# Gate loads of the value stage issued by GpSimd instead of SyncE's queue, in a PEER block on one Trainium2 core

## The chip, the cores and the metric

The kernel runs on one core of a Trainium2 chip. The metric is the device time of one execution in microseconds (us), lower is better. The core has TensorE (PE, matrix products), VectorE (DVE), ScalarE (ACT), GpSimd (POOL) and SyncE (SP). DMAs are issued from the instruction streams of SyncE and GpSimd here, and are carried by the core's 16 DMA engines.

## What is computed

One layer of a hybrid encoder with 512 tokens of width 1024: a token mixer (stick-breaking attention and gated linear attention) and then a PEER channel mixer, whose last part is what the change touches. For each token, 8 heads pick 16 of 128 x 128 single-neuron experts by product keys:

```python
def block(args):
    hb, ib, gb = args
    u = expert_u[ib]
    act = jax.nn.gelu(jnp.einsum('td,thkd->thk', hb, u), approximate=False)
    vv = expert_v[ib]
    return jnp.einsum('thk,thkd->td', gb * act, vv)
```

So y(token) is the sum over its 128 picks of gate x gelu(h . u) x v. The result is gated, added to the residual and normalised.

## The kernel before

The kernel treats the first 128 tokens and the other 384 differently.

**Dense tokens (384).** All 16384 experts are computed for them, in 128 blocks of 128 experts. In the *up stage* block b takes 24 matmuls of 384 columns into one of two banks `ps_u` (`UpProducts.product`); ScalarE empties the bank with a gelu (`gelu`, L1198) into one of four tiles `u_act`, and SyncE stores that tile to DRAM as `activations[b]` (`store`, L1202). gelu(b) waits until the store of block b - 4, from the same tile, has landed. In the *value stage* (`experts`) the activations are loaded again (`load_act`), multiplied on VectorE by the gates (`weigh`, L2049), split into a high and a low part (`w_high` on ScalarE, L2001; `w_low` on VectorE, L2042), and multiplied by the block's rows of v, which are loaded and split too (L1995, L2055): 18 matmuls of 512 columns a block into `ps_y`. The gates of tokens that did not pick an expert are zero.

The gates stand in DRAM as `gate_tiles`. For 256 dense tokens GpSimd spreads them there with 256 indirect DMAs of 128 words each (`spread_gate`, L1467; semaphore `spread`); for the other 128 a one-hot product writes them and SyncE stores them (semaphores `g_stored`). `load_gates(g)` then brings the gates of four blocks (a "quad") into one of two tiles `gates`: 768 KB, 128 partitions x 12 pieces x 512 bytes. gates(g) may be overwritten when quad g - 2 has been weighed (`w_done`).

**Picked rows (the first 128 tokens).** GpSimd fetches, for each of the 128 picks q, one row of u and v for every token by an indirect DMA of 128 rows of 8 KB (`PickedRows.gather`, L1248) into one of four tiles `row`. VectorE takes the dot product with h (L1255), ScalarE the gelu and the gate (L1259, L1262), VectorE adds the weighed v to `y_row` (L1271). gather(q) waits until row q - 4 has been added. The table `ROW_PACE` says in which block of the program each row is used, up to block 248, which is block 120 of the value stage.

**Order.** Every engine runs its own program in order. Steps are counted by b for the up stage and by i = b - 128 for the value stage; step i of VectorE does w_low(i + 1), weigh(i + 2), at most one row, and the split of v(i + 2). The value stage's steps begin at i = -7 (`OPENING`), beside the last up blocks 121 to 127. There SyncE's program interleaves the last u loads and stores with the first loads of v, activations and gates. On GpSimd, spreads and gathers are interleaved by the numbers `SPREAD_AT`, `SPREAD_PACE` and `ROW_BLOCK`; the last spread stands after gather 51, and gathers 52 to 127 follow one another in the same function; the value stage's function for GpSimd is empty.

## Time and profile before

| | |
|---|---|
| median of 3 runs | 1533.53 us (1531.42 to 1534.49) |
| profiled execution, own time | 1531.92 us |
| its span in the trace | 1530.0 us |
| TensorE busy | 1486.6 us (97%) |
| VectorE busy | 1225.9 us (80%) |
| ScalarE busy | 690.9 us (45%) |
| GpSimd busy | 515.9 us (34%) |
| HBM traffic | 278 GB/s over the span |

Busy shares are averages over stages of different kinds: up to about 400 us the mixer and the first keys, then the up stage, and from 993 us on the value stage. Times in the rows are us from the span's start. In a timeline row stand start, length, engine, line, operation and tiles, and in square brackets the engine's idle time before it with what ended it; "issue" is idle time for which the profile shows no releaser. SPq is SyncE's queue of DMA issues: the length there is that of the issue, not of the transfer. Ends of matmuls are modelled, starts are recorded. Software DMAs (q0) are GpSimd's, hardware DMAs (q1) SyncE's.

### The profile page before, as it was taken

Reading aid. Unit: us, or ns where it says so; the run is one execution under the profiler, and the core shown is the slowest. Engines: PE = TensorE matmul, PEld = TensorE weight load, DVE = VectorE, ACT = ScalarE, POOL = GpSimd, SP = SyncE. Lnnn points to the kernel's source line nnn. Section 1 sums busy time; section 2 is a strip of 40 time slices with the busy share of each in tenths; the row PEclk is TensorE's granted clock in tenths of the full one; section 3 lists DMA queues with packets and bytes.
Section 4 is the critical chain, followed back from the end, with each engine's and each line's share of the span. In section 5 each row is a group of like instructions: output and inputs, shape, how many; then the busy total and the mean of one; then the engine's idle time right before and its main releaser. Section 6 shows DMA issues by size and latency. Waiting matters only on the chain.

```text
span 1530.0 us, 22267 instructions
## 1 busy us (share of the span) xinstructions
PE 1486.6 (97%) x7635; PEld 1304.7 (85%) x7635; DVE 1225.9 (80%) x2476; ACT 690.9 (45%) x1189; POOL 515.9 (34%) x439
## 2 busy tenths in 40 slices
PE   6999998999999999999999999999999999999997
PEld 4786666889999999999999999888888888888886
DVE  6775657477799988999988965678888888888887
ACT  5424755363443433434555553344443444434443
POOL 0000000001476777668788867211111111112100
PEclk8999999999999999999999999999999999999999
DMA  9693903045787666756869988999999999999993
GB/s 367 236 352 130 415 29 139 4 144 210 247 277 246 213 223 220 235 181 196 261 222 337 323 327 315 384 377 351 382 373 374 382 361 381 382 369 380 368 349 115
DMA packets 169904, 427.46 MB, mean 279 GB/s; under 512 B 21152, under 2 KB 105280, under 8 KB 149824
## 3 DMA queue, kind: packets, MB, share of 16 engines
q1 hardware_dynamic: 143168, 291.67, 54.8%
q0 software_dynamic: 26624, 134.37, 23.1%
q8 instruction: 61, 1.00, 0.3%
q14 instruction: 51, 0.42, 0.1%
HBM read 373.42 MB, written 52.56 MB: 278 GB/s over the span
## 4 chain that ended last, share of the span: by engine, by line
PE 68%; POOL 4%; DMA 3%; issue 3%; DVE 1%; ACT 0%; DVEq 0%; ACTq 0%; POOLq 0%
PE ps_y L2124 11%; PE ps_y L2126 11%; PE ps_y L2128 11%; PE ps_u L1188 9%; PE ps_u L1190 9%; PE ps_u L1189 9%; POOL gate_tiles L1467 3%; PE ps_q L1475 2%; PE ps_q L1477 2%; PE ps_q L1476 2%; DMA activations<-u_act 1%; DMA row<-in_uv_rows,row_index 1%; PE ps_s L1487 1%; PE ps_g L1821 1%; DMA gate_tiles<-gate_owed,gate_cell 1%
## 5 line engine op out<-in xcount | busy, mean ns | idle before, releaser
L1467 POOL DMA_INDIRECT gate_tiles<-gate_owed,gate_cell x256 | 350.0, 1367 | 129.8 <-issue 72.0
L1188 PE MATMUL ps_u<-h_hi,u_hi 128*128 128x384 f32 x1024 | 349.2, 341 | 7.9 <-ACT u_act L1198 7.6
L1190 PE MATMUL ps_u<-h_hi,u_lo 128*128 128x384 f32 x1024 | 346.6, 338 | 0.0
L1189 PE MATMUL ps_u<-h_lo,u_hi 128*128 128x384 f32 x1024 | 346.5, 338 | 0.0
L1248 POOL DMA_INDIRECT row<-in_uv_rows,row_index x128 | 158.5, 1238 | 510.5 <-DVE y_row L1271 426.6
L1995 ACT CAST v_hi<-v_raw 128x1024 fp32r<-128x1024 f32 x128 | 134.7, 1053 | 266.8 <-DMA v_raw<-in_v 149.8
L2124 PE MATMUL ps_y<-v_hi,w_hi 128*128 128x512 f32 x768 | 238.1, 391 | 0.3 <-DVE w_lo L2042 0.3
L2126 PE MATMUL ps_y<-v_lo,w_hi 128*128 128x512 f32 x768 | 237.4, 390 | 0.0
L2128 PE MATMUL ps_y<-v_hi,w_lo 128*128 128x512 f32 x768 | 237.3, 390 | 0.0
L1188 PEld LDWEIGHTS ps_u<-h_hi,u_hi 128*128 128x128 f32 x1024 | 194.5, 190 | 10.2 <-issue 8.9
L2055 DVE TENSOR_TENSOR v_lo<-v_raw,v_hi 128x1024 fp32r<-128x1024 f32 x128 | 156.2, 1220 | 58.5 <-ACT v_hi L1995 56.1
L1178 DVE TENSOR_TENSOR u_lo<-u_raw,u_hi 128x1024 fp32r<-128x1024 f32 x128 | 154.9, 1217 | 55.0 <-ACT u_hi L1171 52.4
L1189 PEld LDWEIGHTS ps_u<-h_lo,u_hi 128*128 128x128 f32 x1024 | 194.6, 190 | 0.6
L1190 PEld LDWEIGHTS ps_u<-h_hi,u_lo 128*128 128x128 f32 x1024 | 194.4, 190 | 0.0
L1271 DVE SCALAR_TENSOR_TENSOR y_row<-row,row_weights,y_row 128x1024 f32<-128x1024 f32 x127 | 163.0, 1284 | 22.9 <-ACT row_weights L1262 22.9
L1255 DVE CUSTOM_DVE_ANT_0 row<-row,h_row 128x1024 f32<-128x1024 f32 x128 | 155.9, 1218 | 26.8 <-DMA row<-in_uv_rows,row_index 26.6
L2128 PEld LDWEIGHTS ps_y<-v_hi,w_lo 128*128 128x128 f32 x768 | 144.3, 188 | 30.1
L2126 PEld LDWEIGHTS ps_y<-v_lo,w_hi 128*128 128x128 f32 x768 | 144.3, 188 | 29.9
L2124 PEld LDWEIGHTS ps_y<-v_hi,w_hi 128*128 128x128 f32 x768 | 143.5, 188 | 29.6 <-DVE v_lo L2055 0.7
L1198 ACT ACTIVATE u_act<-ps_u 128x384 f32<-128x384 f32 x128 | 62.5, 488 | 199.3 <-PE ps_u L1190 172.3
L1171 ACT CAST u_hi<-u_raw 128x1024 fp32r<-128x1024 f32 x128 | 133.4, 1043 | 2.9 <-DMA u_raw<-in_u 2.9
L366 DVE CUSTOM_DVE_ANT_0 w_ada<-w_ada,c_row 128x1024 f32<-128x1024 f32 x47 | 55.8, 1220 | 0.3 <-DMA w_ada<-in_w_ada 0.3
(321 smaller groups left out, 2074.6 us busy)
## 6 DMA issues: line engine op xcount, KB each, us to landing
u_raw<-in_u SPq DMA_DIRECT2D x128, 512.0 KB, 4.7
v_raw<-in_v SPq DMA_DIRECT2D x128, 512.0 KB, 8.3
activations<-u_act SPq DMA_DIRECT2D x128, 192.0 KB
gates<-gate_tiles SPq DMA_DIRECT2D x32, 768.0 KB, 10.1
w_ada<-in_w_ada SPq DMA_DIRECT2D x23, 1024.0 KB, 8.1
gate_tiles<-blank SPq DMA_DIRECT2D x4, 4096.0 KB, 30.2
act<-activations SPq DMA_DIRECT2D x64, 192.0 KB, 8.6
u_act<-activations SPq DMA_DIRECT2D x64, 192.0 KB, 8.2
```

The lines of the kernel that those rows point to most:

```text
L1178: dve.tensor_tensor(self.lo[n][:], self.raw[n][:], self.hi[n][:].bitcast(F32), ALU.subtract).then_inc(self.lo_done, 1)
L1188: pe.matmul(out, self.hi[n][:, k], hi, start=(k == 0), stop=False)
L1189: pe.matmul(out, self.hi[n][:, k], lo, start=False, stop=False)
L1190: last = pe.matmul(out, self.lo[n][:, k], hi, start=False, stop=(k == KD - 1))
L1248: pool.indirect_dma_start(out=self.row[n][:].rearrange("p a d -> p (a d)"), out_offset=None, in_=self.table, in_offset=bass.IndirectOffset ...
L1255: dve.tensor_tensor_reduce(u, u, h_row[:], 1.0, 0.0, ALU.mult, ALU.add, self.dots[:, q:q + 1]).then_inc(self.dotted, 1)
L1271: dve.scalar_tensor_tensor(self.y[:], v, col, self.y[:], ALU.mult, ALU.add).then_inc(self.added, 1)
L1467: pool.indirect_dma_start(out=g_dram, out_offset=bass.IndirectOffsetOnAxis(ap=picks.cell[:, b, j:j + 1], axis=0), in_=picks.owed[:, b, j:j ...
L2055: dve.tensor_tensor(v_lo[i % VS][:], v_raw[i % VS][:], v_hi[i % VS][:].bitcast(F32), ALU.subtract).then_inc(vlo, 1)
L2124: pe.matmul(out, hi, v_hi[i % VS][:, c], start=first, stop=False)
L2126: pe.matmul(out, hi, v_lo[i % VS][:, c], start=False, stop=False)
L2128: last = pe.matmul(out, lo, v_hi[i % VS][:, c], start=False, stop=end)
```

## The change

`load_gates` moves from SyncE's program to GpSimd's, which now has a function in the value stage: it waits for `g_stored` and for all spreads, and then issues the gathers from 52 on with the 32 gate loads between them. gates(g) stands behind the gathers whose turn (`gather_at`) comes before step 4(g - 1) - 1. SyncE no longer waits for the spreads. The tiles `gates` are allocated ahead of `v_raw` instead of behind `w_lo`. Nothing is computed differently.

```diff
@@ retrieval, gpsimd
-            while q < PICKS:
-                rows.gather(pool, q)
-                q += 1
-
-        def gather_at(q):
-
-            return 7 if q < rows.RING else ROW_BLOCK[q - rows.RING + 1] + 1
+            rows.early = q
@@ PickedRows
+    def gather_at(self, q):
+
+        return 7 if q < self.RING else ROW_BLOCK[q - self.RING + 1] + 1
@@ experts, tiles
+        gates = [sb(f"gates{n}", [P, G_TILES, QUAD, G_TOK]) for n in range(2)]
         v_raw = [sb(f"v_raw{n}", [P, D]) for n in range(VS)]
...
-        gates = [sb(f"gates{n}", [P, G_TILES, QUAD, G_TOK]) for n in range(2)]
@@ experts, sync
-            def load_gates(g):
-                if g >= 2:
-                    sp.wait_ge(w_done, QUAD * (g - 1))
-                src = g_dram.rearrange("(a p i t) o -> p a i (t o)", a=G_TILES, p=P, t=G_TOK)[:, :, g * QUAD:(g + 1) * QUAD]
-                sp.dma_start(gates[g % 2][:], src).then_inc(g_in[g % 2], 16)
-
...
                         for n in range(2):
                             sp.wait_ge(g_stored[n], 16 * (P // G_TOK // 2))
-                        sp.wait_ge(spread, 16 * SPREADS * PEER_HEADS)
-                        load_gates(0)
                         load_v(0)
...
-                    if i == 3 - OPENING:
-                        load_gates(1)
...
-                if i % QUAD == 2 and i + 6 < N_KEYS:
-                    load_gates((i + 6) // QUAD)
@@ experts, gpsimd
-            pass
+            def load_gates(g):
+                if g >= 2:
+                    pool.wait_ge(w_done, QUAD * (g - 1))
+                src = g_dram.rearrange("(a p i t) o -> p a i (t o)", a=G_TILES, p=P, t=G_TOK)[:, :, g * QUAD:(g + 1) * QUAD]
+                pool.dma_start(gates[g % 2][:], src).then_inc(g_in[g % 2], 16)
+
+            for n in range(2):
+                pool.wait_ge(g_stored[n], 16 * (P // G_TOK // 2))
+            pool.wait_ge(spread, 16 * SPREADS * PEER_HEADS)
+            q = rows.early
+            for g in range(N_KEYS // QUAD):
+                while q < PICKS and rows.gather_at(q) < N_KEYS + QUAD * (g - 1) - 1:
+                    rows.gather(pool, q)
+                    q += 1
+                load_gates(g)
+            while q < PICKS:
+                rows.gather(pool, q)
+                q += 1
```

In the rows of order below, a row is an instruction of one engine's program with its line, its tiles and, in brackets, the semaphores it waits for; "x4" is four alike in a row.

SyncE at the opening of the value stage, before: the u load and the store of step -7, and then the first loads of gates, v and activations between the stores of the last blocks.

```order
337 L1163 DMA u_raw<-in_u 128x1024 [waits u_lo_done]
338 L1202 DMA activations<-u_act 128x384 [waits u_act_done]
339 L1938 DMA gates<-gate_tiles 128x12x128 [waits gates_spread,g_stored1,g_stored0]
340 L1932 DMA v_raw<-in_v 128x1024
341 L1202 DMA activations<-u_act 128x384 [waits u_act_done]
342 L1944 DMA act<-activations 128x384 [waits act_stored0]
343 L1944 DMA act<-activations 128x384 [waits act_stored1]
344 L1932 DMA v_raw<-in_v 128x1024
345 L1202 DMA activations<-u_act 128x384 [waits u_act_done]
346 L1932 DMA v_raw<-in_v 128x1024
347 L1202 DMA activations<-u_act 128x384 [waits u_act_done]
348 L1938 DMA gates<-gate_tiles 128x12x128
```

The same place of SyncE's program with the change:

```order
337 L1163 DMA u_raw<-in_u 128x1024 [waits u_lo_done]
338 L1202 DMA activations<-u_act 128x384 [waits u_act_done]
339 L1930 DMA v_raw<-in_v 128x1024 [waits g_stored1,g_stored0]
340 L1202 DMA activations<-u_act 128x384 [waits u_act_done]
341 L1936 DMA act<-activations 128x384 [waits act_stored0]
342 L1936 DMA act<-activations 128x384 [waits act_stored1]
343 L1930 DMA v_raw<-in_v 128x1024
344 L1202 DMA activations<-u_act 128x384 [waits u_act_done]
345 L1930 DMA v_raw<-in_v 128x1024
346 L1202 DMA activations<-u_act 128x384 [waits u_act_done] x4
```

The two gate loads and the wait for `gates_spread` are gone; the store of block 120, row 341 before and 340 now, stands behind the load of v(0) alone.

GpSimd at the end of the spreads, before: the last spreads, then all the gathers that are left.

```order
146 L1467 DMA gate_tiles<-gate_owed,gate_cell 6291456x1 [waits u_mul] x6
147 L1248 DMA row<-in_uv_rows,row_index 128x2048 [waits row_added,row_indexed]
148 L1467 DMA gate_tiles<-gate_owed,gate_cell 6291456x1 [waits u_mul] x2
149 L1248 DMA row<-in_uv_rows,row_index 128x2048 [waits row_added,row_indexed]
150 L1467 DMA gate_tiles<-gate_owed,gate_cell 6291456x1 [waits u_mul] x4
151 L1248 DMA row<-in_uv_rows,row_index 128x2048 [waits row_added,row_indexed] x76
```

The same place with the change, where the gather with five semaphores is gather 52:

```order
149 L1248 DMA row<-in_uv_rows,row_index 128x2048 [waits row_added,row_indexed]
150 L1465 DMA gate_tiles<-gate_owed,gate_cell 6291456x1 [waits u_mul] x4
151 L1248 DMA row<-in_uv_rows,row_index 128x2048 [waits row_indexed,gates_spread,row_added,g_stored1,g_stored0]
152 L1248 DMA row<-in_uv_rows,row_index 128x2048 [waits row_added,row_indexed] x3
153 L1977 DMA gates<-gate_tiles 128x12x128
154 L1248 DMA row<-in_uv_rows,row_index 128x2048 [waits row_added,row_indexed] x2
155 L1977 DMA gates<-gate_tiles 128x12x128
156 L1248 DMA row<-in_uv_rows,row_index 128x2048 [waits row_added,row_indexed] x3
157 L1977 DMA gates<-gate_tiles 128x12x128 [waits mod_kept]
```

Gather 52 now stands behind the wait for the spreads, gates(0) behind gather 55, gates(1) behind gather 57, and from there on a gate load stands behind every two or three gathers. (`mod_kept` is the name that the semaphore of `w_done` first had.)

## Rows read from the trace of the kernel before

**Rows 1.** Windows, value stage: busy us and instructions of each engine, PEclk, DMA share, GB/s.

```profile
1000.00:1500.00 500.00, 500.00 (x2223) 414.33 (x2222) 422.19 (x577) 213.83 (x394) 82.23 (x68) 1.00 1.01 369
```

**Rows 2.** Waits of TensorE, whole program: us in total, times, longest.

```profile
PE ps_u L1188 <- ACT u_act L1198: 7.6, 5, 2.9
```

**Rows 3.** Timeline of TensorE at the stage change.

```profile
965.80 0.42 PE L1188 MATMUL ps_u<-h_hi,u_hi 128*128 128x384 f32 x1 [0.61 <-ACT u_act L1198]
...
978.02 0.34 PE L1189 MATMUL ps_u<-h_lo,u_hi 128*128 128x384 f32 x1
978.19 0.34 PE L1190 MATMUL ps_u<-h_hi,u_lo 128*128 128x384 f32 x1
981.44 0.66 PE L1188 MATMUL ps_u<-h_hi,u_hi 128*128 128x384 f32 x1 [2.91 <-ACT u_act L1198]
...
982.22 0.53 PE L1190 MATMUL ps_u<-h_hi,u_lo 128*128 128x384 f32 x1
...
987.34 0.40 PE L1188 MATMUL ps_u<-h_hi,u_hi 128*128 128x384 f32 x1
...
993.42 0.70 PE L2124 MATMUL ps_y<-v_hi,w_hi 128*128 128x512 f32 x2
```

**Rows 4.** Timeline of ScalarE, gelu(124).

```profile
980.81 0.49 ACT L1198 ACTIVATE u_act<-ps_u 128x384 f32<-128x384 f32 x1 [7.44 <-DMA activations<-u_act]
```

**Rows 5.** Timeline of SyncE's queue: gates(0) and the store of block 120.

```profile
959.41 0.50 SPq L1938 DMA_DIRECT2D gates<-gate_tiles  x1
...
960.77 7.47 SPq L1202 DMA_DIRECT2D activations<-u_act  x1
```

**Rows 6.** Timeline of VectorE: dot of row 52, weigh(0), w_low(0).

```profile
963.48 1.23 DVE L1255 CUSTOM_DVE_ANT_0 row<-row,h_row 128x1024 f32<-128x1024 f32 x1 [5.08 <-DMA row<-in_uv_rows,row_index]
...
982.88 0.56 DVE L2049 TENSOR_TENSOR act<-act,gates 128x384 f32<-128x384 f32 x1 [7.73 <-DMA act<-activations]
...
987.73 0.55 DVE L2042 TENSOR_TENSOR w_lo<-act,w_hi 128x384 fp32r<-128x384 f32 x1
```

**Rows 7.** Timeline of GpSimd: an earlier wait for spreads; last spread, gathers 52 and 55.

```profile
681.88 0.97 POOL L1467 DMA_INDIRECT gate_tiles<-gate_owed,gate_cell  x1 [0.30 <-issue]
687.41 0.97 POOL L1467 DMA_INDIRECT gate_tiles<-gate_owed,gate_cell  x1 [4.56 <-DMA gate_tiles<-gate_owed,gate_cell]
...
952.53 0.97 POOL L1467 DMA_INDIRECT gate_tiles<-gate_owed,gate_cell  x1 [0.30 <-issue]
953.80 1.97 POOL L1248 DMA_INDIRECT row<-in_uv_rows,row_index  x1 [0.31 <-issue]
...
966.69 1.17 POOL L1248 DMA_INDIRECT row<-in_uv_rows,row_index  x1 [7.34 <-DVE y_row L1271]
```

**Rows 8.** Software queue in 954:955 and in 958:959: packets, MB, share of 16 engines.

```profile
q0 software_dynamic: 32, 0.00, 2.4%
...
q0 software_dynamic: 10, 0.08, 24.3%
```

**Rows 9.** TensorE after two other waits; windows, columns as in rows 1.

```profile
952.48 0.41 PE L1188 MATMUL ps_u<-h_hi,u_hi 128*128 128x384 f32 x1 [1.64 <-ACT u_act L1198]
...
812.79 0.41 PE L1188 MATMUL ps_u<-h_hi,u_hi 128*128 128x384 f32 x1 [2.13 <-ACT u_act L1198]
...
814.00:815.00 1.00, 1.00 (x5) 1.00 (x5) 1.00 (x2) 0.91 (x1) 0.70 (x2) 0.50 0.85 125
```

**Rows 10.** By tile: landing of gate loads 940:1000; gate loads and gathers, value stage.

```profile
DMA to landing us min/median/max: 15.1/16.2/16.4
...
L1938 SPq DMA_DIRECT2D gates<-gate_tiles x29: 371/432/1122, 1016.5 to 1477.1; - x29
...
DMA to landing us min/median/max: 7.5/9.7/13.1
...
L1248 POOL DMA_INDIRECT row<-in_uv_rows,row_index x68: 936/1175/1972, 999.9 to 1469.2; - x68
...
DMA to landing us min/median/max: 7.2/8.9/10.9
```

More of the change, by code:

```diff
@@ L1446, in gpsimd @@
                     at = SPREAD_AT + SPREAD_PACE * g + (SPREAD_PACE - SPREAD_REST) * n / SPREADS
-                    while q < PICKS and gather_at(q) < at + (SPREAD_REST if n == 0 else 0):
+                    while q < PICKS and rows.gather_at(q) < at + (SPREAD_REST if n == 0 else 0):
                         rows.gather(pool, q)
```

## The prediction, before the changed kernel was run

> **What bounds the kernel now.** I read the windows first, then the waits of TensorE, then the timeline of each engine around the only place where TensorE still stands still. In the value stage TensorE is busy in 500.00 of 500 us at full clock, and the DMA engines are busy too (share 1.01) [rows 1]. So moving issues between queues can give nothing there; it can only take, if something comes so late that TensorE waits. Over the whole program, the longest wait of TensorE for one releaser is 7.6 us in five pieces, all for the gelu that empties a bank of the up products; the longest piece is 2.9 us [rows 2]. It lies where the up products end and the value products begin, and there the timeline shows three losses [rows 3]: 0.61 us before block 123 (965.80), 2.91 us before block 126 (981.44), and behind the second a half clock. Matmuls that start every 0.17 us at 978.02 to 978.19 start every 0.32 us at 982.22. From 981.44 to 987.34 there are 18 matmuls in 5.90 us, where 18 x 0.173 = 3.12 would do: 2.78 us lost. The first value product starts at 993.42.
>
> Who is late at block 126? gelu(124) starts at 980.81 after 7.44 us of idle time, for a store of activations [rows 4]: the ring of four makes it wait until block 120 is stored. The queue of SyncE shows why [rows 5]: gates(0) is issued at 959.41, and the store of block 120, which stands two places behind it, has an issue of 7.47 us. An issue of a plain load there is 0.4 us at the median [rows 10]. 768 KB in pieces of 512 bytes stand ahead of that store.
>
> The 0.61 us before block 123 have another cause. VectorE waits 5.08 us for row 52, until 963.48 [rows 6]; ScalarE stands in its own order behind that dot product, and gelu(121) behind ScalarE's step. TensorE starts 965.80 - 963.48 = 2.32 us after the row is in.
>
> **The change, part by part.** (1) SyncE no longer issues the 32 gate loads and no longer waits for the spreads; its wait for the dense gates' stores (`g_stored`) stays. At the stage change v(0) and the store of block 120 then go out from 959.4 on, with no 768 KB ahead of them. I take the 2.91 us wait and the 2.78 us of half clock behind it as gone: 5.7 us is all there is to win. Cover is ample: without the gates the store has from about 960 to 978 to land.
>
> (2) GpSimd now waits for `g_stored` and for all 256 spreads before gather 52, where it had gone straight on: the last spread starts at 952.53 and gather 52 at 953.80 [rows 7]. When is the last spread in? Earlier waits of this kind ended 5.53 us after the last spread's start (681.88 to 687.41); that gives 958.1, 4.3 us late. The queue of the software DMAs gives an earlier bound: it moves 32 packets of almost no bytes in 954 to 955, and the next ones, 8 KB each, are row 52's in 958 to 959 [rows 8], so the spread's data has gone by 955. I let its completion count 0.6 us behind that (my choice between nothing and the 3.1 us left to 958.1, near the low end because the packets are what is seen), and gather 52 goes out at about 955.6, 1.8 us late. I take row 52 in 1.4 us late, since its packets then share the engines with less, and keep 4.3 as the other end. Behind gather 52 stand 53, 54, 55 and gates(0); behind its landing stand VectorE's dot, ScalarE, gelu(121) and block 123. So the 0.61 us wait becomes 2.0.
>
> (3) Does a wait of 2.0 us halve the clock? After 1.64 us (952.48) it did not; after 2.13 us (812.79) it did, to 0.50 in 814 to 815 [rows 9]; after 2.91 us it did. So the place is open between 0 and 2.8 us. I take 1.0, a little under the middle.
>
> (4) gates(0) now stands behind gather 55. That waits for row 51's add and started at 966.69 [rows 7]; 1.4 us later and 1.2 + 0.3 us long, it lets gates(0) go at 969.6, where SyncE sent it at 959.41. Landing took 15.1 to 16.4 us at the stage change and 9.7 us at the median later [rows 10]: 979.3 to 986.0. From weigh(0) at 982.88 to the end of w_lo(0) at 988.28 VectorE takes 5.4 us [rows 6], so the first value product can start at 984.7 to 991.4. TensorE, by (1) to (3), is there at 993.4 - 5.7 + 1.4 + 1.0 = 990.1. Hidden for most of the range, so nothing is charged; at the late end it costs 1.3 us.
>
> (5) Price of issuing a gate load on GpSimd. The trace has no plain load on that engine. A load is 128 x 12 pieces of 512 bytes. From below: a gather of 128 rows is 1.175 us [rows 10]. From above: twelve times that, 14.1 us, if time follows the number of pieces. I take 5 us, nearer the gather: a spread of 128 single words takes 0.97 us, a gather of 128 rows of 8 KB 1.17 us [rows 7], so bytes hardly count and a fixed share is likely; how much of the 1.2 us grows with pieces stays open. In the value stage GpSimd is busy 82.23 us of 500 with 68 gathers [rows 1]; with 0.3 us between instructions 397 us are free for the 29 loads of that stretch, 13.7 us each. At 5 us it all lies beside other work.
>
> (6) Rows behind a gate load. A gather lands in 8.9 us [rows 10] and its dot product comes three rows of the pace later, some 20 us; 5 us of issue and about 4 us of a gate load's data ahead of it in the same queue still fit. Nothing charged. SyncE's loads of v no longer stand behind gates, which is worth nothing either, as TensorE waits for none of them.
>
> Sum: -2.91 - 2.78 + 1.4 + 1.0 = -3.3 us. Against the profiled execution's own 1531.92 us that is 1528.6; the median of the runs is 1533.53, 1.6 above it, so 1530.2 us is the forecast, 0.21% less. From no change a measurement of this kernel can tell about 0.2%, 3.1 us.
>
> **Rivals.** *The gain is given back at block 123 or is not there.* If row 52 comes 4.3 us late, the wait becomes 4.9 us with the whole half clock behind it: -5.7 + 4.3 + 2.8 = +1.4 us, 1534.9. Or the store lands late anyway, because the same bytes share the same 16 engines: then -0 + 1.4 to 2.4. Against that speaks that the issue itself was held for 7.47 us [rows 5]. The trace thus has a queue effect beside the sharing of engines. The Trainium skill (DMA: Bandwidth & Descriptors, section Issuing engines are not separate DMA queues) says that DMAs of all issuing engines interleave on the same 16 engines and that spreading them saves only the issue time, usually small; by that rule the result would be this rival, about 1534. The half way between forecast and this rival (whole half clock at block 123, row 1.8 late) gives -1.1 us, 1532.4.
>
> *GpSimd becomes the bound* (slower). If a gate load costs 14.1 us there, the stretch of 500 us needs 29 x 14.4 + 68 x 1.48 = 518 us: +18, less the 3.3, so 1548. It decides from 13.7 us a load. For it speaks that nothing in the trace shows so many pieces generated in software; against it, the fixed share in (5). The Trainium skill (SBUF — State Buffer, section Summary: rules for kernel authors) advises against this move: descriptors written by GpSimd starve while VectorE runs in its wide modes. VectorE is busy 422 us of 500 here [rows 1], yet 68 gathers had a median of 1175 ns and a maximum of 1972 [rows 10], so I see the starvation at 0.8 us at most.
>
> *gates(0) comes too late* (slower, milder). If generation takes 10 us and landing 11.5 us behind it (between the 9.7 and the 16.4 of [rows 10]), gates(0) is in at 969.6 + 21.5 = 991.1 and the first value product starts 5.4 us later, at 996.5, with a half clock behind a wait of 6 us: 996.5 - 993.4 + 2.8 = +5.9 us, 1539.
>
> *More than forecast.* No half clock at block 123 and row 52 hardly late: -5.7 + 1 = -4.7, down to 1527.
>
> **How the numbers follow.** Forecast as summed (gain 2.2 to 4.4 us): 0.42, of it 0.25 beyond 0.2%. More than that: 0.12. Given back or not there: 0.25. gates(0) too late: 0.09. GpSimd the bound: 0.12. Faster 0.25 + 0.12 = 0.37; same 0.17 + 0.25 = 0.42; slower 0.21. The range of the forecast alone is 1529 to 1531.5. The range that holds 8 in 10 goes from 1527 (all the gain but the row's delay) to 1538, short of the case in which GpSimd is the bound and of the worst of late gates.
>
> **What the changed profile would show.** Right: the store of block 120 issued in under 1.5 us; gelu(124) waiting for TensorE and no longer for a store; no wait of TensorE before block 126; gather 52 some 2 us behind its old place after the last spread and a wait of about 2 us before block 123; gate loads on GpSimd of some 5 us; the first value product about 3 us before 993.4; 500 of 500 us busy in the value stage. Wrong: TensorE waiting in the value stage for w_lo or v_lo; GpSimd busy over 90% there; gate loads near 1 us would not change the sum, near 14 would. The forecast also falls if the wait before block 123 grows past 3 us.

## The result, and the profile after

The change made the kernel slower: 1540.03 us at the median (1530.15 to 1545.18, 20 runs) against 1532.18 us (1524.27 to 1535.67, 20 runs), ratio 1.0045 with the interval 1.0031 to 1.0059. That is about 6.9 us (4.8 to 9.0) more, where 3.3 us less were forecast. 1540.03 lies above the range of 1527 to 1538. The profiled execution of the changed kernel took 1536.13 us, with a span of 1534.3 us (before 1530.0); it lies below the median of its kernel, so this trace need not show all of the 6.9 us. Here and below two executions of e14, of 1852 and 5243 us, are left out of the ratio.

The windows and TensorE's waits of the changed kernel, value stage first (busy us of PE, PEld, DVE, ACT, POOL; clock; DMA share; GB/s):

```profile
1000.00:1500.00 500.00, 496.29 (x2203) 410.04 (x2202) 423.35 (x575) 212.92 (x394) 113.46 (x98) 1.00 1.00 367
```

```profile
PE ps_u L1188 <- ACT u_act L1198: 8.8, 4, 5.5
...
PE ps_y L2127 <- DVE w_lo L2045: 4.0, 4, 2.6
```

The reader should see two things. TensorE, busy 500.00 of 500 us in [rows 1], now stands still for 3.7 us in the value stage, and the waits have a name, `w_lo`. The waits for gelu at the change of stages have grown from 7.6 to 8.8 us [rows 2], where they should have shrunk.

The timeline of the changed kernel at the change of stages, by engine (start, duration, what, idle time before it):

```profile
951.56 2.04 POOL L1465 DMA_INDIRECT gate_tiles<-gate_owed,gate_cell  x1 [0.30 <-issue]
958.97 0.98 POOL L1248 DMA_INDIRECT row<-in_uv_rows,row_index  x1 [5.37 <-issue]
...
970.60 1.18 POOL L1248 DMA_INDIRECT row<-in_uv_rows,row_index  x1 [8.13 <-DVE y_row L1275]
971.78 1.10 POOL L1977 DMA_DIRECT2D gates<-gate_tiles  x1
...
967.39 1.23 DVE L1259 CUSTOM_DVE_ANT_0 row<-row,h_row 128x1024 f32<-128x1024 f32 x1 [10.03 <-DMA row<-in_uv_rows,row_index]
...
981.89 0.56 DVE L2052 TENSOR_TENSOR act<-act,gates 128x384 f32<-128x384 f32 x1 [2.83 <-DMA gates<-gate_tiles]
...
958.72 0.50 SPq L1202 DMA_DIRECT2D activations<-u_act  x1
...
969.72 0.66 PE L1188 MATMUL ps_u<-h_hi,u_hi 128*128 128x384 f32 x1 [5.47 <-ACT u_act L1198]
...
973.67 0.34 PE L1188 MATMUL ps_u<-h_hi,u_hi 128*128 128x384 f32 x1
...
993.21 0.70 PE L2127 MATMUL ps_y<-v_hi,w_hi 128*128 128x512 f32 x2
```

The last spread starts at 951.56 and gather 52 only at 958.97, 7.4 us later; in [rows 7] it was 1.3 us. Row 52 is in at 967.39 instead of 963.48 [rows 6], gelu(121) stands behind it, and TensorE waits 5.47 us before block 123, with the granted clock at 0.50 in 970 to 973 (the lower level, 1.2 GHz) and short spacing again from 973.67. The other side of the exchange is there as well: the store of block 120 is issued in 0.50 us instead of 7.47 [rows 5], and no wait stands before block 126. Both together leave the first value product where it was, 993.21 against 993.42 [rows 3].

So the 4.3 us between the two profiled executions lie behind that point. From the first value product to the end of the span: 1534.3 - 993.21 = 541.1 us, before 1530.0 - 993.42 = 536.6 us. I call this the **tail** below. The loads of gates in the value stage, by their line:

```profile
L1977 POOL DMA_DIRECT2D gates<-gate_tiles x30: 1067/1084/1098, 1002.8 to 1482.2; - x30
...
DMA to landing us min/median/max: 7.5/11.3/12.9
```

One costs GpSimd 1.08 us, and they are in after 11.3 us at the median (9.7 in [rows 10]). VectorE never waits for them in this stretch. What comes late is something else. The queues of 1000 to 1500 us (packets, MB, share of the 16 engines), first of the changed kernel, then of the kernel before:

```profile
q0 software_dynamic: 16032, 94.90, 51.0%
q1 hardware_dynamic: 35188, 88.13, 48.2%
```

```profile
q1 hardware_dynamic: 82147, 112.78, 65.4%
q0 software_dynamic: 9792, 71.31, 35.1%
```

The same bytes go in far fewer packets. Over the whole program the hardware queue loses 143168 - 93504 = 49664 packets and the software queue gains 33280 - 26624 = 6656: by load and engine 97 packets before, 13 now, that is 96 packets of 512 bytes and one of 4 bytes before, and now 12 packets of 4096 bytes and one of 4 bytes by the sizes in the packet records: eight pieces of 512 bytes travel as one packet. And ScalarE, which casts v, waits for v more (us in total, times, longest; changed, then before):

```profile
ACT v_hi L1998 <- DMA v_raw<-in_v: 179.1, 68, 5.1
ACT v_hi L1998 <- PE ps_y L2131: 47.7, 31, 2.2
```

```profile
ACT v_hi L1995 <- DMA v_raw<-in_v: 149.8, 55, 5.4
ACT v_hi L1995 <- PE ps_y L2128: 76.6, 47, 2.2
```

Read the second row of each pair as spare time. Where the cast waits for TensorE to free a buffer, v is early. Where it waits for the transfer, v is late, and three buffers must cover it. In the kernel before 55 casts found v late; now 68 do. This is how it reaches TensorE, in the chain of waits of the changed kernel around its longest new wait:

```profile
1278.16 13.06 DMA v_raw<-in_v
...
1291.24 0.02 ACT v_hi L1998
...
1294.37 1.22 DVE v_lo L2058
1295.59 0.48 DVE w_lo L2045
1296.07 0.14 issue
1296.20 0.70 PE ps_y L2127 x2
```

And this is what GpSimd had put into the engines around the issue of that load of v:

```profile
1271.28 1.17 POOL L1248 DMA_INDIRECT row<-in_uv_rows,row_index  x1 [3.25 <-DVE y_row L1275]
1272.44 1.08 POOL L1977 DMA_DIRECT2D gates<-gate_tiles  x1
1277.77 1.21 POOL L1248 DMA_INDIRECT row<-in_uv_rows,row_index  x1 [4.24 <-DVE y_row L1275]
```

A load of v took 13.06 us, where the median is 8.3 in both kernels. TensorE had no product to do for 2.59 us.

### The profile page after: what moved, and what is told of

Read it like the earlier page. It is cut to its first block and busy times, and to the rows that moved or that the text cites. A ratio compares the mean times of both kernels' runs of the same rounds, so it can differ in the third digit from the quotient of the medians.

```text
span 1534.3 us, 22268 instructions
## 1 busy us (share of the span) xinstructions
PE 1486.0 (97%) x7635; PEld 1302.8 (85%) x7635; DVE 1227.6 (80%) x2476; ACT 690.3 (45%) x1189; POOL 547.2 (36%) x471
## 3 DMA queue, kind: packets, MB, share of 16 engines
q1 hardware_dynamic: 93504, 266.51, 48.8%
q0 software_dynamic: 33280, 159.54, 28.5%
## 6 DMA issues: line engine op xcount, KB each, us to landing
gates<-gate_tiles POOLq DMA_DIRECT2D x32, 768.0 KB, 11.3
```

## The experiments

All were timed in five rounds beside the kernel before. In each profile, one by kernel, I read the tail, and how long ScalarE waited for v between 1000 and 1500 us. Theory A says that the loss comes from two places and mostly from the value stage; theory B that it comes from gather 52 at the change of stages.

### The change taken apart

**e1_wait_later.** The changed kernel; GpSimd's waits stand behind gathers 52 to 55.

```diff
-            for n in range(2):
-                pool.wait_ge(g_stored[n], 16 * (P // G_TOK // 2))
-            pool.wait_ge(spread, 16 * SPREADS * PEER_HEADS)
             q = rows.early
...
+                if g == 0:
+                    for n in range(2):
+                        pool.wait_ge(g_stored[n], 16 * (P // G_TOK // 2))
+                    pool.wait_ge(spread, 16 * SPREADS * PEER_HEADS)
                 load_gates(g)
```

> The changed kernel, with GpSimd's waits for the spreads and the dense gates' stores moved behind gathers 52 to 55, right ahead of gates(0). Theory A (two places: the late gather 52 eats the gain at the stage change, and the value stage loses some 8 us on its own because gate loads in GpSimd's queue hold up the loads of v): gather 52 goes out 1 to 2 us after the last spread again, the wait before block 123 is back under 1 us, the first value product starts at about 988, and the total is some 5 us under the changed kernel's 1540, near 1535, 0.2% above before. Theory B (one place: the late row 52 is the whole loss and whatever follows is its echo): about 1527, 0.3% below before.

Measured: 1537.92 us, ratio 1.0036 (1.0015 to 1.0056); tail 542.3.

```profile
960.16 0.66 PE L1188 MATMUL ps_u<-h_hi,u_hi 128*128 128x384 f32 x1 [6.40 <-ACT u_act L1198]
...
960.22 2.04 POOL L1465 DMA_INDIRECT gate_tiles<-gate_owed,gate_cell  x1 [0.30 <-issue]
962.56 1.98 POOL L1248 DMA_INDIRECT row<-in_uv_rows,row_index  x1 [0.31 <-issue]
```

Gather 52 is free again, 2.3 us behind the last spread, and before block 123 TensorE waits 0.23 us, as theory A said. The wait of 6.40 us is another one: it stands before block 120 and ends before the last spread is issued, so the place of GpSimd's waits can't have made it. With it the first value product comes at 997.24 and not at 988. The time decides nothing between "0.2% above before" and the change's 0.45%: the interval holds both. Theory B's 1527 us is out.

**e2_wait_only.** The kernel before, with the wait for the spreads ahead of gather 52 and nothing else.

```diff
+            pool.wait_ge(spread, 16 * SPREADS * PEER_HEADS)
             while q < PICKS:
                 rows.gather(pool, q)
```

> The kernel before, with nothing but GpSimd's wait for all spreads put ahead of gather 52; the gate loads stay with SyncE. Theory A: gather 52 is 5 us late, TensorE waits some 5 us before block 123 with a half clock behind it, the store's delay before block 126 partly hides behind that; 3 to 6 us above before, 1535 to 1538, and TensorE still busy 500 of 500 us in the value stage. Theory B: the whole loss, 1540, with waits in the value stage.

Measured: 1534.10 us, ratio 1.0005 (0.9990 to 1.0020); tail 536.6. The wait alone costs nothing that can be measured, where theory A had 3 to 6 us for it: gather 52 went 2.4 us behind the last spread, not 5 us late, and TensorE does not wait before block 123. In this execution it waits 4.78 us at 954.80, again before block 120 and ahead of gather 52 (956.13), and later only 0.34 and 0.65 us where the kernel before waited 2.91. It looks as if a wait early in the change of stages took the place of a later one, but this early wait is not the edit's.

**e3_first_two.** Gates 0 and 1 and the waits as in the change; loads 2 to 31 stay in SyncE's loop.

```diff
-            for g in range(N_KEYS // QUAD):
+            for g in range(2):
...
+                if i % QUAD == 2 and i + 6 < N_KEYS:
+                    load_gates((i + 6) // QUAD)
```

> The change at the stage change alone: GpSimd waits for the spreads ahead of gather 52 and issues gates(0) and gates(1); the other 30 gate loads stand in SyncE's program as before (the two kinds on semaphores of their own). Theory A: the stage change is neutral, about 1532 as before, and TensorE is busy 500 of 500 us from 1000 on. Theory B: 1540, as the changed kernel.

Measured: 1535.61 us, ratio 1.0014 (0.9992 to 1.0036); tail 536.5. That may be nothing or up to 0.36%.

**e4_later_thirty.** The other half alone: change of stages as before, loads 2 to 31 taken out of SyncE's loop and put into GpSimd's.

```diff
-                if i % QUAD == 2 and i + 6 < N_KEYS:
-                    load_gates((i + 6) // QUAD)
...
+            for g in range(2, N_KEYS // QUAD):
+                while q < PICKS and rows.gather_at(q) < N_KEYS + QUAD * (g - 1) - 1:
+                    rows.gather(pool, q)
+                    q += 1
+                load_gates(g)
```

> The other part alone: gates(0) and gates(1) from SyncE as before, no wait of GpSimd for the spreads, and the 30 gate loads from gates(2) on from GpSimd between its gathers. Theory A: the stage change is as before (first value product at 993), and the value stage loses some 8 us, 1540. Theory B: 1532, no loss.

Measured: 1537.18 us, ratio 1.0035 (1.0019 to 1.0052); tail 539.1; TensorE waits for `w_lo` again (2.0 us), and ScalarE waits 182 us for v. Most of the loss is in these thirty loads, though theory A's 8 us were too many: the ratio is worth 5.4 us, of which this profiled execution (1533.39 us, near the lowest of its kernel) shows 2.5 in the tail. Theory B has fallen.

### What in the thirty loads

**e5_gate_early** (changed kernel; a gate load one gather earlier):

```diff
-rows.gather_at(q) < N_KEYS + QUAD * (g - 1) - 1
+rows.gather_at(q) < N_KEYS + QUAD * (g - 1) - (3 if g >= 2 else 1)
```

> From the changed kernel, every gate load from the third on is issued one row fetch earlier, as soon as its buffer is free, instead of right behind a row fetch of the same stretch. Theory C (the loss lies in the value stage, where a row fetch and a gate load issued within about 1.2 us of each other fill the software queue together and hold back the loads of v): apart from each other they disturb less; from the first value product to the end of the span takes 537 to 538.5 us instead of 541.1, value stage TensorE busy 498.5 or more of 500, time 1533 to 1535 us. Rival D (any gate load in the software queue costs, wherever it is put, by its share of the DMA engines): 540 to 542 us from first value product to the end, time 1537 to 1540.

Measured: 1538.49 us, ratio 1.0026 (1.0010 to 1.0042); tail 541.9; waits for v 189 us. Tail and time are those of rival D. Theory C has fallen in this form: it is not that a gather and a gate load stand side by side.

**e6_gates_on_act** (kernel before; loads 2 to 31 at the end of ScalarE's step, in its hardware queue):

```diff
+                if i >= 1 and i % QUAD == 1 and i + 7 < N_KEYS:
+                    load_gates((i + 7) // QUAD)
```

> From the kernel before, gate loads 2 to 31 are issued from ScalarE's hardware queue, behind the work of every fourth block; gates 0 and 1 stay in SyncE's queue. Theory E (what hurts is that the gate load runs beside the loads of v instead of between them in one queue): as bad as the changed kernel, 539 to 542 us from the first value product to the end, time 1536 to 1540. Theory F (what hurts is the software queue that the gate loads share with the rows, or the way it packs 512-byte pieces): no loss, 536.5 to 537 us, 1532 to 1534 us. Under both ScalarE gives about 0.1 to 1 us for each issue, 3 to 30 us of its spare time.

Measured: 1535.35 us, ratio 1.0007 (0.9993 to 1.0020); tail 536.6. (Its profiled execution was one of the longest of its twelve, by waits at the change of stages.) ScalarE's waits and the third queue, 1000 to 1500 us:

```profile
ACT v_hi L1999 <- PE ps_y L2134: 140.8, 68, 2.5
...
ACT v_hi L1999 <- DMA v_raw<-in_v: 60.5, 24, 4.6
```

```profile
q10 hardware_dynamic: 46560, 23.59, 17.3%
```

A queue of its own does not harm. The pieces stay single here, 46560 / 30 / 16 = 97 packets by load and engine, and the load takes 17.3% of 500 us, 2.88 us of each engine. On GpSimd the same load takes less, (51.0 - 35.1)% of 500 / 30 = 2.65 us. Still v is waited for 60 us here and 179 there; the gates themselves are late instead (13.3 us to landing), and they can afford it. Theory E has fallen; F holds.

**e7_order_on_sync** (kernel before; gates 0 and the wait for the spreads moved behind the second loads, all on SyncE, with the gate buffers placed as in the change):

```diff
-                        sp.wait_ge(spread, 16 * SPREADS * PEER_HEADS)
-                        load_gates(0)
                         load_v(0)
...
                         load_v(1)
+                        sp.wait_ge(spread, 16 * SPREADS * PEER_HEADS)
+                        load_gates(0)
```

> From the kernel before, all loads stay on SyncE; the wait for the spreads and the load of gates 0 move behind the load of v 0, the store of block 120 and the loads of act 0, act 1 and v 1. Theory A (TensorE's waits at the change of stages before blocks 123 and 126 stand in for each other; what is left there is worth 1 to 3 us once nothing else is added): the wait before block 126 goes, one before block 123 of 0.5 to 3 us stays, value stage unchanged at 536.6 us from first value product to the end; time 1530.5 to 1533.5. Rival G (gates 0 then comes too late for the first value blocks): first value product 1 to 4 us later, 1534 to 1537.

Measured: 1535.18 us, ratio 1.0005 (0.9989 to 1.0021); tail 536.6. The time is in rival G's range and not in A's. The wait before block 126 is gone, but the gates only stand in the way of the next store, that of block 121, and TensorE waits before block 127 instead:

```profile
972.57 13.83 SPq L1202 DMA_DIRECT2D activations<-u_act  x1
...
993.42 0.42 PE L1188 MATMUL ps_u<-h_hi,u_hi 128*128 128x384 f32 x1 [3.85 <-ACT u_act L1198]
```

So this kernel does not test the gain of 5.7 us; it shows a second time, after [rows 5], that a store behind gates in SyncE's queue is held. It does settle one thing: with the gate buffers where the change has them it loses nothing, and e4 loses with the buffers where the kernel before has them, so their place is not the cause.

**e8_gate_halves** (changed kernel; every load in two of 384 KB, apart):

```diff
+                part = slice(half * G_TILES // 2, (half + 1) * G_TILES // 2)
...
+                for half in range(2):
+                    while ... < N_KEYS + QUAD * (g - 1) + ((-3, 0)[half] if g >= 2 else -1):
```

> From the changed kernel, each gate load is two of 6 tiles (384 KB each), issued apart: the first half early, the second behind the next row fetches. GpSimd issues 64 of them, at about 0.6 to 1.1 us each. Theory C (bursts): 537 to 539 us from first value product to the end, 1533 to 1536 us. Rival D (share of the DMA engines, whatever the size): 540 to 542 us, 1537 to 1540. If the issue of a half costs as much as a whole (1.08 us), GpSimd is busy some 30 us more of the value stage, without reaching its limit.

Measured: 1538.37 us, ratio 1.0019 (1.0005 to 1.0033); tail 536.5; waits for v 81 us. The tail of the one profiled execution is whole again, the time is not: it lies in rival D's range. I took what is left of the loss for the part at the change of stages; e10 below tests that.

**e9_act_long_pieces and e12_pool_long_pieces** (thirty loads on ScalarE or on GpSimd, read from a contiguous 768 KB of v, so that the gates of these blocks are not the reference's):

```diff
-src = g_dram.rearrange("(a p i t) o -> p a i (t o)", ...)[:, :, g * QUAD:(g + 1) * QUAD]
+src = io["v"].rearrange("k p d -> (k p d)")[g * P * QUAD * DENSE:(g + 1) * P * QUAD * DENSE]
+     .rearrange("(p a i t) -> p a i t", p=P, a=G_TILES, i=QUAD)
```

> The variant with gate loads 2 to 31 in ScalarE's hardware queue (it kept 536.6 us from first value product to the end), with each load read from a contiguous 768 KB of v, a stand-in of the same size, in place of the scattered pieces of 512 bytes: the gates of these blocks are then not the reference's. Theory P (what harms in the software queue is the size of the packets: against a 4 KB packet of gates each 4 KB packet of v waits about 8 times as long as against one of 512 bytes): 538.5 to 542 us from first value product to the end although the loads take less engine time, v landing at its slowest later than 12.8 us, waits for w_lo of 2 us or more. Rival S (it is the software queue itself, or that the rows stand in the same queue): 536.6 us, no waits for w_lo beyond the 0.3 us of before. Between: both.

> The variant with gate loads 2 to 31 on GpSimd (539.1 us from first value product to the end, +0.35%), with the same contiguous stand-in as source: the gates of these blocks are then not the reference's. If the software queue's packets of 512-byte pieces already run like long ones, about the same packets and times as that variant: 538.5 to 541 us, +0.2 to +0.4%. Gathering 512-byte pieces also costs DMA time that this leaves out (2.65 us of engine time a load now; a load of v of 512 KB says what long pieces take); if it is this time that harms: 536.6 us, and no change from the kernel before. GpSimd's instruction falls well under 1.08 us if its price goes by the number of pieces (128 in place of 1536).

Measured: e9 1530.41 us, ratio 0.9992 (0.9974 to 1.0010), tail 536.8, waits for v 30 us. e12 1530.63 us, ratio 1.0000 (0.9977 to 1.0022), tail 536.5, waits for v 49 us; GpSimd's instruction falls to 0.58 us. The queues of e12, 1000 to 1500 us, and ScalarE's wait:

```profile
q1 hardware_dynamic: 35959, 90.07, 49.0%
q0 software_dynamic: 14119, 94.92, 47.1%
```

```profile
ACT v_hi L2005 <- DMA v_raw<-in_v: 48.9, 19, 4.7
```

The same queue and the same bytes as e4 in packets that are longer still (4320 for 30 loads: by load and engine eight of 6144 bytes and one of 4), and no loss. So neither the software queue as such nor the length of its packets is enough; theories P and S have fallen as I wrote them. What is less is the time: (47.1 - 35.1)% of 500 / 30 = 2.0 us of each engine by load instead of 2.65.

**e13_pool_scattered_v and e14_pool_2k_pieces** (as e12, the first `src` in pieces of 512 bytes at the strides of the real gates, the second in pieces of 2 KB; again a stand-in for these gates):

```diff
+table = io["v"].rearrange("k p d -> (k p d)")[0:G_TILES * G_CELLS]
+src = table.rearrange("(a p i t) -> p a i t", a=G_TILES, p=P, t=G_TOK)[:, :, g * QUAD:(g + 1) * QUAD]
+src = table[0:G_TILES * G_CELLS // 4].rearrange("(b p g e) -> p b g e", b=3, p=P, g=8)[:, :, g % 8]
```

> The variant with gate loads 2 to 31 on GpSimd, each read from v as a stand-in, but in the same 1536 pieces of 512 bytes at the same strides as the real gates (the gates of these blocks are then not the reference's). The contiguous stand-in cost nothing (536.5 us from first value product to the end). If it was the short scattered pieces in the software queue that harm: ScalarE's waits for v back at 170 us or more, 538.5 to 542 us from first value product to the end, GpSimd's instruction 1.08 us, ratio 1.002 to 1.004. If it was where the gates lie in memory: 536.5 us, waits of 50 to 80 us, ratio 1.000.

> The same with 384 pieces of 2 KB in place of 1536 of 512 bytes. If what harms is the DMA time of short pieces: as contiguous, 536.5 to 537 us from first value product to the end, waits for v of 50 to 110 us, ratio 0.999 to 1.001, GpSimd's instruction between 0.58 and 1.08 us. If any scattered source harms: 538.5 us or more.

Measured: e13 1540.68 us, ratio 1.0042 (1.0025 to 1.0060); e14 1536.02 us, ratio 0.9998 (0.9981 to 1.0016), tail 536.6, instruction 0.80 us. ScalarE's wait for v in e13:

```profile
ACT v_hi L2006 <- DMA v_raw<-in_v: 176.6, 68, 4.6
ACT v_hi L2006 <- PE ps_y L2139: 47.4, 35, 2.6
```

The loss is back with the short pieces, wherever they lie, and gone with 2 KB (84 us of waits for v). Both send the same number of packets, 32864 in the software queue over the whole program, of the same bytes; the pieces of 2 KB only take less time, by the packet records 0.16 us instead of 0.21 for one of 4096 bytes, or 2.1 us of each engine by load instead of 2.6. One part of the expectation failed: the profiled execution of e13, its shortest, has a tail of 536.6, although its waits for v are those of the slower kernels. Late v makes a loss likely, not certain, in a single execution.

**e10_later_halves and e11_halves_together** (thirty loads on GpSimd in halves, change of stages as before; apart, or right behind each other, where the pair in the last line is (-1, -1)):

```diff
-while q < PICKS and rows.gather_at(q) < N_KEYS + QUAD * (g - 1) - 1:
+while q < PICKS and rows.gather_at(q) < N_KEYS + QUAD * (g - 1) + (-3, 0)[half]:
```

> Change of stages as before, gate loads 2 to 31 on GpSimd in halves of 384 KB issued apart. The two places then both cost nothing: 536.5 us from first value product to the end, ratio 0.999 to 1.001, 1533 to 1535 us. If the ratio stays near the 1.0019 of the halves in all loads, that kernel's loss is not at the change of stages, and the division of the loss into two places is wrong.

> As the variant with halves issued apart, but both halves right behind each other where the whole load stood. If the length of the burst harms (768 KB in the software queue at once): 538.5 to 541 us from first value product to the end, as with whole loads. If the size of one load harms (what one issue puts into the queue): 536.5 to 537 us. GpSimd is busy about 30 us more than with whole loads if a half costs as much as a whole, as the halves apart showed about 0.8 us for each.

Measured: e10 1534.53 us, ratio 1.0015 (0.9996 to 1.0035), tail 539.5, waits for v 197 us. e11 1530.29 us, ratio 0.9999 (0.9979 to 1.0020), tail 536.6, waits for v 75 us. Together cost nothing, so the length of the burst is not the cause. But the loads of e11 have the same pieces, the same queue and the same packets of 4096 bytes as those of e4, and take (50.2 - 35.1)% of 500 / 30 = 2.5 us of each engine where e4 takes 2.6: what differs in the program is that two instructions issue what one did. So short pieces in the software queue are not enough for the loss either, and why a division in two removes it is open.

e10 was the test of the division of the loss into two places, and it did not confirm it: the ratio is nearer to e8's 1.0019 than to 1, its interval holds both, TensorE waits 1.5 us for `w_lo`, and the waits for v are the longest of all (in e8 81 us). Halves apart can cost in the value stage, so e8's +0.19% can't be put down to the change of stages alone.

### The change of stages once more

**e16_first_two_rest_act** (as e3, loads 2 to 31 in ScalarE's queue):

```diff
-                if i % QUAD == 2 and i + 6 < N_KEYS:
-                    load_gates((i + 6) // QUAD)
+                if i >= 1 and i % QUAD == 1 and i + 7 < N_KEYS:
+                    load_gates((i + 7) // QUAD)
```

> Gates 0 and 1 and the wait for the spreads on GpSimd as in the change, the other 30 loads in ScalarE's hardware queue. A third look at what the change costs at the change of stages alone: 536.6 us from first value product to the end; if that part of the loss is real, as the two kernels before it suggest (+0.14%, +0.19%), a ratio of 1.001 to 1.003; if it is nothing, 0.999 to 1.001.

Measured: 1538.05 us, ratio 1.0018 (1.0004 to 1.0032), tail 536.6. With e3 (1.0014) this is the second kernel that has the change's part at the change of stages and gate loads behind it that cost nothing elsewhere (e6, the kernel before): about +0.16%, 2.5 us, of which only this one is clear of nothing. GpSimd's timeline here repeats what the changed kernel showed:

```profile
959.02 1.96 POOL L1465 DMA_INDIRECT gate_tiles<-gate_owed,gate_cell  x1 [0.30 <-issue]
965.82 0.98 POOL L1248 DMA_INDIRECT row<-in_uv_rows,row_index  x1 [4.84 <-issue]
```

6.8 us from the last spread to the next gather; 7.4 in the changed kernel, 6.2 in e3, 6.7 in e8, but 3.0 in e5, which has the same program there.

All kernels, by the two places:

| kernel | gates 0, 1 | gates 2 to 31 | ratio to before | waits for v, us | tail, us |
|---|---|---|---|---|---|
| before | SyncE | SyncE | 1 | 150 | 536.6 |
| e2 | SyncE, wait on GpSimd | SyncE | 1.0005 | 150 | 536.6 |
| e7 | SyncE, later | SyncE | 1.0005 | 106 | 536.6 |
| e6 | SyncE | ScalarE | 1.0007 | 60 | 536.6 |
| e9 | SyncE | ScalarE, contiguous | 0.9992 | 30 | 536.8 |
| e12 | SyncE | GpSimd, contiguous | 1.0000 | 49 | 536.5 |
| e14 | SyncE | GpSimd, 2 KB | 0.9998 | 84 | 536.6 |
| e11 | SyncE | GpSimd, halves together | 0.9999 | 75 | 536.6 |
| e10 | SyncE | GpSimd, halves apart | 1.0015 | 197 | 539.5 |
| e4 | SyncE | GpSimd | 1.0035 | 182 | 539.1 |
| e13 | SyncE | GpSimd, 512 B of v | 1.0042 | 177 | 536.6 |
| e3 | GpSimd | SyncE | 1.0014 | 112 | 536.5 |
| e16 | GpSimd | ScalarE | 1.0018 | 98 | 536.6 |
| e8 | GpSimd, halves | GpSimd, halves apart | 1.0019 | 81 | 536.5 |
| e5 | GpSimd | GpSimd, earlier | 1.0026 | 189 | 541.9 |
| e1 | GpSimd, wait later | GpSimd | 1.0036 | 179 | 542.3 |
| change | GpSimd | GpSimd | 1.0045 | 179 | 541.1 |

No version beats the kernel before. Even e9, with the cheapest loads of all, only equals it, since TensorE is busy 500 of 500 us in the value stage as before. The waits for v are those of one execution each: before, e2, e7 and e3 have the same value stage and show 150, 150, 106 and 112 us. TensorE's own waits for `w_lo` between 1000 and 1500 us are 3.7 us in the changed kernel, 3.9 in e1, 2.6 in e5, 1.8 in e4, 1.5 in e10 and none in any other.

## Why the prediction was wrong

**The step that failed is the first one**, and (6) repeats it. "So moving issues between queues can give nothing there; it can only take, if something comes so late that TensorE waits" was right; but I then charged nothing for it: "SyncE's loads of v no longer stand behind gates, which is worth nothing either, as TensorE waits for none of them." I looked at TensorE's waits, which were none, and not one link back. ScalarE waited 150 us for v in the kernel before, in 55 casts, and only in 47 for TensorE: little was in reserve, and it could have been read. It is on the thirty loads of the value stage that e4 and e13 put +0.35% and +0.42%, 5.4 and 6.4 us: the larger part of the 6.9 us. With the 2.5 us of the change of stages that makes 8 to 9, at the upper end of the interval. That late v carries the loss to TensorE is seen in five profiles, 2.5 to 5.7 us longer in the tail; in e13, whose executions are 6.4 us longer, the profiled one shows none of it.

What takes the reserve, by the runs, is thirty whole loads of 512-byte pieces in the software queue (e4, e13), and each of three steps away from that removes the loss: longer pieces (e12, e14), ScalarE's hardware queue (e6), or each load in two halves behind each other (e11). What the three have in common is not shown. It is not the engine time alone (2.9 us a load in e6, 2.5 in e11), and not the length of a packet alone: by the packet records one of the gates lasts 0.21 us in e4 and 0.23 us in e12, which loses nothing. The Trainium skill (DMA: Bandwidth & Descriptors, section Queues, rings and completion order) says that each DMA engine takes turns between its queues, one whole packet at a time. e4 against e6 fits that: in ScalarE's queue a packet of gates that goes between two of v lasts 2.88 us / 97 = 0.03 us, in the software queue 2.65 us / 13 = 0.2 us. By this rule the gates yield to v in e6 and v to the gates in e4, as the landings show (gates 13.3 and 11.2 us, v 7.5 and 8.4 us at the median). e12 does not fit it by itself: there the packets of the gates are longer still, and v lands after 7.0 us. That the turns are part of the mechanism is argued; no run shows the order of packets in one engine. The Trainium skill's other rule on the same page, which I weighed for the change of stages (Issuing engines are not separate DMA queues: spreading DMAs over issuing engines saves only issue time), told more of the truth than my sum: in the time nothing was won. It does not tell that something can be lost.

**(1) The gain of 5.7 us.** The mechanism is confirmed: store of block 120 issued in 0.50 us, no wait before block 126. In the profiled execution the gain was given back by (2) and (3): 4.9 us more of waiting before block 123 and 1.9 us of half clock, 0.9 us less before block 120. Whether other executions had 5.7 us to give is doubtful. Of the kernels whose change of stages is untouched, the profiled executions take 77.2 us (e10) to 93.9 us (e6) from the last one-hot matmul to the first value product, 84.2 in the kernel before, and their waits stand at different blocks. Before block 120 TensorE waits 4.3 to 6.4 us in e1, e2, e5, e8, e9, e12, e13 and e16, where the kernel before shows 1.64, always ahead of gather 52 and so not made by what the variants change behind it; in these eight the wait before block 126 is at most 0.94 us instead of 2.91. I subtracted a wait of one execution as if it were fixed.

**(2) Gather 52.** Taken 1.8 us late with 4.3 as the other end; it was 7.4 us behind the last spread instead of 1.3, so 6.1 us late. The queues in the changed kernel, 956 to 957 us, show the spread's packets:

```profile
q1 hardware_dynamic: 160, 0.38, 96.7%
q0 software_dynamic: 30, 0.00, 2.2%
```

In [rows 8] they went at 954 to 955, 1.5 to 2.5 us after the spread's start. Here 30 go at 956 to 957 and the last two at 957 to 958, about 5 us after it, among transfers of the hardware queue that fill the engines. The last packet starts at 957.55 and gather 52 at 958.97, 1.4 us behind it (0.7 in e2), where I had chosen 0.6. (The dense gates' stores were not what it waited for: the last was issued at 909.82.) So the step failed less where I saw the doubt, between packets and completion, than before it: the packets themselves came late. The spread's instruction took 2.04 us, not 0.97 as in [rows 7], and by the time it was over the hardware queue was moving again. In the variant with the wait alone the engines were free of the hardware queue at 955 to 956:

```profile
q0 software_dynamic: 32, 0.00, 2.4%
```

There gather 52 started at 956.13, 2.4 us after its last spread (953.72), and in e5 3.0 us after it; in e3, e8 and e16 it was 6.2, 6.7 and 6.8 us, as in the changed kernel. The wait before block 123 became 5.47 us, not 2.0. A late row 52 needs no wait for the spreads, though: in e4 and e14, where GpSimd goes straight on, TensorE waits 3.61 and 4.20 us there. **(3)** The half clock came: 12 products in 3.95 us (969.72 to 973.67), where 12 x 0.173 = 2.08 would do, 1.9 us lost between my 1.0 and the 2.8 at the upper end. What the change costs here, 2.5 us by two ratios, is not settled further. From the start of block 121 to the first value product the four kernels with the late gather take 36.8 us on average (34.6 to 37.7), the nine with an untouched change of stages 34.5 (31.6 to 36.9), and e5, with the change but a gather that is not late, 29.9: that fits, within a scatter of 5 us. The wait alone (e2) costs nothing that can be measured, with its gather early, and e1, with the waits behind the gathers, is faster than the change by less than the intervals.

**(4) gates(0)** went at 971.78, and VectorE waited 2.83 us for it, until 981.89. First value product at 993.21: hidden, as forecast, but without room.

**(5) The price on GpSimd** is 1.08 us, just under the lower bound of 1.175 and not 5. By e12, e14 and the whole load it goes up slowly with the pieces: 0.58 us for 128, 0.80 for 384, 1.08 for 1536. "Gate loads near 1 us would not change the sum" held.

**The rivals.** That GpSimd becomes the bound and that gates(0) comes too late did not happen. The gain given back at block 123 did, in the profiled execution in full, and is the smaller part of the loss. The larger part was none of my rivals, though the list of signs had it ("TensorE waiting in the value stage for w_lo or v_lo"): I named the sign and gave it no chance. (The low end of my range was a slip besides: 1533.5 - 4.7 is 1528.8 and not 1527.)

## What to carry to other kernels

Where TensorE is busy all the time and the DMA engines are too, read the reserve one link further back: how often does the engine that takes a transfer wait for the transfer, and how often for a free buffer? When the first outnumbers the second, a rearrangement of queues can cost, and a term for it belongs in the sum. In this kernel a background load of 512-byte pieces was free in a hardware queue, and on GpSimd it was free in pieces of 2 KB or more. And don't subtract a wait of one execution before you know that others have it: two or three profiles of the same stretch would have shown 77 to 94 us where I counted on tenths.

## What was not expected of the hardware

- A plain load with 1536 pieces costs GpSimd 1.08 us by the trace, less than a gather of 128 rows (1.175 us).
- GpSimd's queue packs eight pieces of 512 bytes into one packet of 4096 bytes (13 packets instead of 97 by load and engine, one of them of 4 bytes).
- In the software queue pieces of 512 bytes cost each engine 2.65 us for 768 KB, 2 KB 2.2 us (e14: (49.0 - 35.6)% of 500 / 30, for the 69 gathers of its window), 6 KB 2.0 us. The packet records themselves sum to 2.6, 2.1 and 1.9 us (e4, e14, e12).
- The almost empty packets of a scatter took from under 2.5 us to about 5 us to go out, the latter with the hardware queue at 90 to 97% of the engines when they went.
